# Latent products on unshifted input, with the shift's row added by matmuls, and new orders in conv norm, gathers and the last up unit

## What is computed

```
ada = silu(c) @ w_ada + b_ada;  sh_m, sc_m, ... = split(ada, 6)     # rows of 1024
h   = rmsnorm(x, g) * (1 + sc_m) + sh_m
cq, ckv, k_rope, fq, fk, fv, f_logit, g_mla, g_fox = split(h @ w_in)
q = rmsnorm(cq) @ w_uq;  kv = rmsnorm(ckv) @ w_ukv                   # the latents, 384 and 256 wide
```

## Time and profile before

| | us |
|---|---|
| median of 3 runs (lowest, highest) | 1018.14 (1015.21, 1019.87) |
| the profiled execution | 1018.16 |
| its span, first to last instruction | 1016.4 |
| TensorE matmuls busy | 965.3 (95%) |
| VectorE (DVE) busy | 465.0 (46%) |
| ScalarE (ACT) busy | 378.7 (37%) |
| mean granted TensorE clock | 0.986 |
| read from memory | 307.31 MB, 303 GB/s over the span |

### The profile page before, as it was taken

The page is one execution under the profiler, slowest core; times in us unless marked ns, Lnnn a source line. Parts: engine busy times, 40 slices in busy tenths (PEclk is TensorE's granted clock), DMA queues, the critical chain, the costliest instruction groups (busy, mean ns, idle before and its releaser), DMA issues.

```text
span 1016.4 us, 15018 instructions
## 1 busy us (share of the span) xinstructions
PE 965.3 (95%) x6185; PEld 668.1 (66%) x6185; DVE 465.0 (46%) x858; ACT 378.7 (37%) x718; POOL 27.4 (3%) x60
## 2 busy tenths in 40 slices
PE   6899999998999999999989899999999999998997
PEld 3698777898999999987988534343434443332433
DVE  1787666575688468757784411212121212111113
ACT  2455545464666356553672422121211121111211
POOL 1000000000000000002121000000000000000000
PEclk9999999999999999989999999999999999999999
DMA  9967733452655445444575599999999999999996
GB/s 386 390 261 268 293 153 158 173 241 83 247 193 216 175 166 193 173 173 166 189 310 232 226 428 429 426 428 427 427 430 427 427 428 427 429 426 427 428 427 269
DMA packets 23397, 309.34 MB, mean 304 GB/s; under 512 B 2592, under 2 KB 3104, under 8 KB 4000
## 3 DMA queue, kind: packets, MB, share of 16 engines
q1 hardware_dynamic: 23184, 307.32, 74.1%
q10 hardware_dynamic: 144, 1.05, 0.3%
HBM read 307.31 MB, written 1.05 MB: 303 GB/s over the span
## 4 chain that ended last, share of the span: by engine, by line
PE 79%; DMA 14%; DVE 5%; issue 1%; ACT 1%; POOL 0%; DVEq 0%; SPq 0%
PE ps L996 76%; DMA ring<-experts 4%; DMA work<-experts 4%; DMA slot<-experts 4%; DMA ring<-dense 2%; DVE wl L1638 1%; PE ps L1194 1%; PE ps L1565 1%; DVE ring L1722 0%; PE ps L1507 0%; DVE xT L2065 0%; DVE wb L2142 0%; ACT wh L577 0%; PE ps L1159 0%; PE ps L1319 0%
## 5 line engine op out<-in xcount | busy, mean ns | idle before, releaser
L996 PE MATMUL ps<-hH,wh 128*128 128x256 f32 x704 | 201.3, 286 | 4.0 <-DVE hL L1662 1.9
L1638 DVE TENSOR_TENSOR wl<-ring,wh 128x1024 fp32r<-128x1024 f32 (+1 forms) x136 | 163.9, 1215 | 85.2 <-ACT wh L577 84.8
L996 PE MATMUL ps<-hL,wh 128*128 128x256 f32 x704 | 198.9, 283 | 0.0
L996 PE MATMUL ps<-hH,wl 128*128 128x256 f32 x704 | 198.8, 282 | 0.0
L577 ACT ACTIVATE wh<-ring 128x1024 fp32r<-128x1024 f32 (+1 forms) x136 | 140.8, 1044 | 125.3 <-PE ps L996 99.3
L996 PEld LDWEIGHTS ps<-hH,wh 128*128 128x128 f32 x704 | 134.6, 191 | 6.1 <-issue 3.7
L996 PEld LDWEIGHTS ps<-hL,wh 128*128 128x128 f32 x704 | 134.4, 191 | 0.0
L996 PEld LDWEIGHTS ps<-hH,wl 128*128 128x128 f32 x704 | 134.2, 191 | 0.0
L2334 DVE SCALAR_TENSOR_TENSOR wc<-wc,w_slot,ps 128x512 f32<-128x512 f32 x16 | 12.0, 747 | 220.9 <-PE ps L996 220.9
L996 PE MATMUL ps<-aH,wh 128*128 128x256 f32 x304 | 86.1, 283 | 5.9 <-DVE wb L2190 2.6
L996 PE MATMUL ps<-aL,wh 128*128 128x256 f32 x304 | 85.3, 281 | 0.0
(11 more groups left out here) (349 smaller groups left out, 1419.4 us busy)
## 6 DMA issues: line engine op xcount, KB each, us to landing
ring<-dense SPq DMA_DIRECT2D x39, 2048.0 KB, 8.1
ring<-experts SPq DMA_DIRECT2D x28, 2048.0 KB, 27.8
slot<-experts SPq DMA_DIRECT2D x28, 2048.0 KB, 28.9
work<-experts SPq DMA_DIRECT2D x20, 2048.0 KB, 28.2
early<-experts SPq DMA_DIRECT2D x10, 2048.0 KB, 26.5
wb<-experts SPq DMA_DIRECT2D x9, 2048.0 KB, 25.2
early<-dense SPq DMA_DIRECT2D x4, 2048.0 KB, 9.2
ring<-dense SPq DMA_DIRECT2D x4, 1024.0 KB, 4.7
```

The lines of the kernel that those rows point to most:

```text
L996: return nc.tensor.matmul(o_, l, r, start=start, stop=stop, skip_group_check=True)
L1638: V.tensor_tensor(wl[:, c % CHUNKS, 0:n], src, wh[:, c % CHUNKS, 0:n].bitcast(F32), ALU.subtract)\
```

## The change

- The shift's ada items are loaded after cq and ckv. These two are multiplied with the parts of n_t without the shift, which go to aH and aL; the shift's ada products are done between ckv's chunks. Then shift_product multiplies the shift's columns with the raw weights of cq and of ckv (in four groups of columns), ACT copies the row (shift_row), and shift_add multiplies it with a matrix of ones into the accumulators, which adds the sum over the four groups to every token. The slots of cq and ckv are kept until then.
- fq accumulates in banks 4 and 5, and the shifted hH and hL are made beside the first chunks of fq. DVE's order of ada steps and splits is new up to uq1: the last two steps of ada12 come after uq1's split.
- Scale's and shift's ada products use four groups of 256 columns instead of two of 512, and half the columns are copied and turned.
- Conv norm: the product with the gate, the squares, their mean and the spread come earlier in the orders of DVE, ACT and TensorE; the last w2o_attn chunk stands behind the spread.
- The fourth gather is done after unit 0; unit 93 is loaded in two transfers, each with half the rows of every product, and the second half of it is awaited only in the middle. Two semaphores are merged into one (dve_setup).

```diff
+LAST_UP = PER_PASS - 3
...
+SHIFT_STEPS = {"cq": 1, "ckv": 3}
...
-    for nm, c0, k0, kn, slot in (("scale0", D, 0, 4, None), ("scale1", D, 4, 4, None), ("shift0", 0, 0, 4, 4),
-                                 ("shift1", 0, 4, 2, 5), ("shift2", 0, 6, 2, TAIL)):
+    def ada_cols_item(nm, c0, k0, kn, slot=None):
         item(f"ada_{nm}", kn, D, [("w_ada", k0, c0, D)], 0, None, slot)
+
+    ada_cols_item("scale0", D, 0, 4)
+    ada_cols_item("scale1", D, 4, 4)
     in_item("cq", 0)
     in_item("ckv", 2)
-    in_item("fq", 0)
+    ada_cols_item("shift0", 0, 0, 4, 4)
+    ada_cols_item("shift1", 0, 4, 2, 5)
+    ada_cols_item("shift2", 0, 6, 2, TAIL)
+    in_item("fq", 4)
...
+        shift_rows = {"cq": wa[:, 2048:2048 + Q_RANK], "ckv": wa[:, 2048 + Q_RANK:2048 + CKQ + HEADS]}
...
+            def half_k(v, i):
+                return v.rearrange("p (j n) -> p j n", j=2)[:, :, 1024 * i:1024 * i + 1024]
+
             def load_unit(u):
-                if u < PER_PASS - 1:
+                if u == LAST_UP:
+                    for i in range(2):
+                        sp.dma_start(half_k(unit(u), i), half_k(W["experts"][u], i))\
+                            .then_inc(unit_loaded(u, 0)[0] if i else S(f"slot{TAIL}_loaded"), 16)
...
+                    if before["name"] in SHIFT_STEPS:
+                        sp.wait_ge(S("shift_steps"), SHIFT_STEPS[before["name"]])
...
-                if i == 0:
-                    act.wait_ge(S("ada_cols"), 1)
-                norm_high(0, adaT[:, SH_M:SH_M + KD], 2 * i, 2 * i + 2)
+                for k in (2 * i, 2 * i + 1):
+                    act.wait_ge(S("norm_t"), k + 1)
+                    nc.scalar.activation(aH[:, k, :], n_t[:, k, :], ACT.Copy).then_inc(S("norm_high"), 1)
             split("ckv")
-            split("fq", 0, 2)
+            split("fq", 0, 1)
+
+            def shift_row(name, steps):
+                act.wait_ge(S("shift_steps"), steps)
+                nc.scalar.activation(shift_rows[name], ps[:, 7, 0:IT[name]["n"]], ACT.Copy).then_inc(S("shift_row"), 1)
+
+            act.wait_ge(S("ada_cols"), 1)
+            norm_high(0, adaT[:, SH_M:SH_M + KD], 0, 4)
+            split("fq", 1, 2)
+            shift_row("cq", 1)
+            norm_high(0, adaT[:, SH_M:SH_M + KD], 4, 8)
+            split("fq", 2, 3)
+            shift_row("ckv", 3)
+            split("fq", 3)
 
             act.wait_ge(S("lat_copied"), 4)
...
-            split("fq", 2)
...
+            act.wait_ge(S("cy_ready"), 2)
+            nc.scalar.activation(csq, cy, ACT.Square).then_inc(S("cv_sq"), 1)
             o2_out(2)
             squares_o2(3)
             split("w2o_attn", 2, 3)
-            act.wait_ge(S("cy_ready"), 2)
-            nc.scalar.activation(csq, cy, ACT.Square).then_inc(S("cv_sq"), 1)
...
-            def ada_half(name, row):
+            def ada_half(name, c0):
 
                 it = IT[f"ada_{name}"]
                 pe.wait_ge(S(f"slot{it['slot']}_loaded"), it["loaded"])
                 w = slot_view(it)
                 for kk in range(it["kn"]):
                     k = it["srcs"][0][1] + kk
-                    for q in range(2):
-                        r = 32 * (row + q)
-                        ins = mm(ps[r:r + 1, 7, :], cact[:, k:k + 1], w[:, kk, 512 * q:512 * q + 512], k == 0, k == KD - 1)
+                    for q in range(4):
+                        ins = mm(ps[32 * q:32 * q + 1, 7, c0:c0 + 256], cact[:, k:k + 1], w[:, kk, 256 * q:256 * q + 256],
+                                 k == 0, k == KD - 1)
                 ins.then_inc(S("ada_used"), 1)
 
             def turn_half(i):
                 pe.wait_ge(S("ada_row"), i + 1)
-                for s in range(4):
-                    r = slice(64 * i, 64 * i + 64)
-                    ins = nc.tensor.transpose(ps[:, 6, 256 * i + 64 * s:256 * i + 64 * s + 64], ada_row[r, s * P:s * P + P],
-                                              ident[r, r])
+                for s in range(2 * i, 2 * i + 2):
+                    ins = nc.tensor.transpose(ps[:, 6, s * P:s * P + P], ada_row[:, s * P:s * P + P], ident[:])
                 ins.then_inc(S("ada_turned"), 1)
...
-            pe.wait_ge(S("bank7_zero"), 1)
+            pe.wait_ge(S("dve_setup"), 1)
             ada_half("scale0", 0)
             norm_totals(0, 5)
             ada_half("scale1", 0)
             norm_spread("norm_rstd", 1, rstd, 4)
             turn_half(0)
-            for i in range(3):
-                ada_half(f"shift{i}", 2)
+
+            def shift_product(name):
+
+                it = IT[name]
+                for k in range(KD):
+                    q = k % 4
+                    ins = mm(ps[32 * q:32 * q + 1, 7, 0:it["n"]], adaT[:, SH_M + k:SH_M + k + 1], slot_view(it)[:, k, :],
+                             k < 4, k >= 4)
+                ins.then_inc(S("shift_steps"), 1)
+
+            def shift_add(name, count):
+
+                it = IT[name]
+                pe.wait_ge(S("shift_row"), count)
+                for tt in range(TT):
+                    ins = mm(ps[:, it["acc"] + tt, 0:it["n"]], ones, shift_rows[name], False, True)
+                ins.then_inc(S("shift_steps"), 1)
+
+            linear("cq", aH, aL, True, ready=("norm_in", [IN_BASE[0] + k + 1 for k in range(KD)]))
+            pe.wait_ge(S("c_steps"), 3)
+            chunk("ckv", 0, aH, aL, True)
+            ada_half("shift0", 256)
+            chunk("ckv", 1, aH, aL, True)
+            ada_half("shift1", 256)
+            ada_half("shift2", 256)
+            chunk("ckv", 2, aH, aL, True)
             turn_half(1)
-
-            linear("cq", hH, hL, True, ready=("norm_in", [IN_BASE[0] + k + 1 for k in range(KD)]))
-            pe.wait_ge(S("c_steps"), 3)
-            linear("ckv", hH, hL, True)
-            pe.wait_ge(S("lat_copied"), 2)
-            linear("fq", hH, hL, False)
-            pe.wait_ge(S("lat_copied"), 4)
-            pe.wait_ge(S("fz_in"), 1)
+            chunk("ckv", 3, aH, aL, True)
+            h_in = ("norm_in", [IN_BASE["shifted"] + k + 1 for k in range(KD)])
+            pe.wait_ge(S("ada_cols"), 1)
+            shift_product("cq")
+            chunk("fq", 0, hH, hL, False, ready=h_in)
+            shift_add("cq", 1)
+            shift_product("ckv")
+            chunk("fq", 1, hH, hL, False, ready=h_in)
+            shift_add("ckv", 2)
+            for ci in range(2, 4):
+                chunk("fq", ci, hH, hL, False, ready=h_in)
+            pe.wait_ge(S("lat_copied"), 5)
             linear("fk", hH, hL, False)
+            linear("fv", hH, hL, True)
...
+            chunk("w2o_attn", 3, aH[:, 4:8], aL[:, 4:8], False, 0, True, False, o_in)
...
+                    if u == LAST_UP:
+                        pe.wait_ge(S(f"slot{TAIL}_loaded"), base_loaded[TAIL] + p * 16 + 16)
+                    else:
+                        pe.wait_ge(*unit_loaded(u, p))
                     w = unit(u)
                     for kk in range(4):
                         k = 4 * half + kk
+                        if u == LAST_UP and kk == 2:
+                            pe.wait_ge(*unit_loaded(u, p))
...
+                    if u == 0:
+                        gather(0, 3, FIRST_BANKS[3])
 
             def put(tt, c0, n, bank):
 
...
-                for i in range(4):
+                for i in range(3):
...
-                r = slice(64 * i, 64 * i + 64)
                 dve.wait_ge(S("ada_used"), count)
-                V.tensor_copy(ada_row[r], ps[r, 7, :]).then_inc(S("ada_row"), 1)
+                V.tensor_copy(ada_row[:, 256 * i:256 * i + 256], ps[:, 7, 256 * i:256 * i + 256]).then_inc(S("ada_row"), 1)
...
-            half_out(1, IT["ada_shift2"]["ada"]).then_inc(S("ada_cols"), 1)
-            dve.wait_ge(S("ada_cols"), 1)
             for i in range(4):
                 split("cq", i, i + 1)
                 for k in (2 * i, 2 * i + 1):
                     dve.wait_ge(S("norm_high"), IN_BASE[0] + k + 1)
+                    V.tensor_tensor(aL[:, k, :], n_t[:, k, :], aH[:, k, :].bitcast(F32), ALU.subtract).then_inc(S("norm_in"), 1)
+            split("ckv")
+            split("fq", 0, 1)
+            half_out(1, IT["ada_shift2"]["ada"]).then_inc(S("ada_cols"), 1)
+            dve.wait_ge(S("ada_cols"), 1)
+            for i in range(4):
+                for k in (2 * i, 2 * i + 1):
+                    dve.wait_ge(S("norm_high"), IN_BASE["shifted"] + k + 1)
                     V.scalar_tensor_tensor(out=hL[:, k, :], in0=n_t[:, k, :], scalar=adaT[:, SH_M + k:SH_M + k + 1],
                                            in1=hH[:, k, :].bitcast(F32), op0=ALU.add, op1=ALU.subtract).then_inc(S("norm_in"), 1)
-            split("ckv", 0, 2)
+                if i < 3:
+                    split("fq", i + 1, i + 2)
+            dve.wait_ge(S("shift_steps"), 2)
+            for tt in range(TT):
+                V.tensor_copy(cqkv[:, tt, 0:Q_RANK], ps[:, IT["cq"]["acc"] + tt, 0:Q_RANK]).then_inc(S("lat_copied"), 1)
             dve.wait_ge(S("c_steps"), 3)
```

(49 more changed lines are left out.)

19 lines of the change are left out of this document (8 added, 11 removed).

## The result

The changed kernel took 1028.57 us by the median of four runs (1026.17 to 1031.60), the kernel before beside it 1018.67: 1.0122 times as long, with a 95% interval of 1.0097 to 1.0147. The forecast was 1023.2, the range ended at 1028.0. The profiled execution is the shortest of the four, 1026.17 us with a span of 1024.4, so 8.0 longer than the profile before; the medians are 9.9 apart. This gap between profile and median turns out to matter.

What follows compares the result with a forecast made beforehand. The prediction took the chain of waits to end in the stream of expert weights, moved by any delay upstream of unit 0. 2.0 + 8.5 - 0.4 - 2.9 - 0.95 - 1.2 = +5.05 on 1018.16: 1023.2 us, range 1013.5 to 1028.

Steps and rivals of the forecast that it cites:

- part 2: DVE order: ada(1,2)'s last steps behind uq1's split issue ada13, ukv1 and g0 late: +8.5 us, 0.4 given back.
- part 1: Start: cq begins 9.3 us earlier, but 11.3 us are added on TensorE before fv's end: +2.0 us there.
- part 3: Conv norm: cy is multiplied earlier on DVE, so w2o_conv starts earlier: -2.9 us (-1.5 to -4).
- part 4: Gathers: gather 3 moves behind unit 0, so unit 0 ends and the weight stream restarts earlier: -0.95 us.
- added on TensorE up to fv's end, clock left out: Before fv's end: shift products 3.7, turn 0.4, new products and adds 4.7, fk 0.85 us.
- clock after the gap: TensorE idles from about 22.7 to 27.6 us ahead of cq; the lower clock then loses 1.6 us.
- Rival 1: Loads from 92 to 112 us: the late ada13 is covered, the DVE-order term nearly vanishes; 1015 us, chance 0.13.
- rival 3: ada13, ukv1, g0 and ada20 share the queue's rate, ada13 comes 3 to 5 us later; 1026 to 1028, chance 0.15.
- fk's wait: Before fv's end: DVE copies latents after the shift's addition, so fk's split is late: 0.85 us, between 0 and 2.
- cq ran at full rate after near idle: Lower bound of 0 for the clock loss ahead of cq, from 3 us of near idle at 34 to 36.9 us.
- Part 5: Last up unit: it lands in halves, TensorE starts earlier, unit 94's landing then limits: -1.2 us (0 to -1.6).

Runs made afterwards that it cites:

- ada12_early: The changed kernel with the last two ada(1,2) steps directly behind the first two, ahead of uq0's and uq1's splits: 1020.98 us, ratio 1.0036 to the kernel before.
- last_alone: The kernel before with only the last up unit's load in halves: 1016.42 us against 1017.71, ratio 0.9997.
- conv_alone: The kernel before with the conv-norm change alone: 1016.02 us against 1017.71, ratio 0.9985.
- four_groups_conv_last: The kernel before with ada products on four column groups, the conv-norm change and the last up unit in halves: 1012.97 us against 1017.03, ratio 0.9962.
- gather_alone: The kernel before with only gather 3 moved behind unit 0: 1016.41 us against 1017.71, ratio 0.9994.
- after_again: The changed kernel run once more without an edit: 1027.63 us against 1017.40 for the kernel before, ratio 1.0099.

## Why the prediction was right and wrong

The mechanism of the largest term was right, and so was its size: part 2 decides, the end goes the slow way. What failed are sizes in the other parts, all to the same side: the start (part 1) came out at +4.8 us instead of +2.0, conv norm (part 3) at -1.1 instead of -2.9, the gathers (part 4) at +0.4 instead of -0.95.

| term | forecast | measured |
|---|---|---|
| cq's first matmul | 27.6 | 26.6 to 29.7, mean of four 28.1 |
| the same against before | -9.3 | -7.2 (before: mean of five 35.3) |
| added on TensorE up to fv's end, clock left out | 9.65 | 10.6 (59.72 less 49.1) |
| clock after the gap | 1.6 | 1.7 to 2.7 (61.4 to 62.4 less 59.72) |
| fv's end | +2.0 | +2.4 by the two profiles, +4.8 by the means (90.18 of three, 85.36 of five) |
| ada13, ukv1, g0 late | +8.5 - 0.4 | +8.1 (40.17 less 32.10) |
| conv norm | -2.9 | -1.84, and +0.75 at the gathers |
| gather 3 | -0.95 | +0.4 |
| last up unit | -1.2 | -0.9 |

- **Part 2** came out step by step. Forecast and the profile after: ada13 issued near 95 and at 95.41, DVE's wait 5 to 6 and 5.75 us, g0 ready for ACT at about 109.5 and at 109.37, its first matmul near 112.5 and at 112.52. From fv's end to that matmul it was 8.1 us more than before (24.13 against 16.05), where 8.5 was forecast. ada12_early takes most of it back. The rule on ring order that the prediction took from the Trainium skill, "DMA: Bandwidth & Descriptors", section "Queues, rings and completion order", speaks of the order in which descriptors are taken up, not of landing; "can't pass" said more than it. The landings did keep the order: ada13 was there for DVE at 103.22, ukv1 for ACT at 104.50, g0 at 109.37. Rival 1 is out, and rival 3 too: ada13 did not come later than 8 us after its issue.
- **Part 1** is the largest miss, 2.8 us at fv's end by the means, and it has three pieces. The first, 1.8 us, is the sum of the added work and the clock, forecast at 11.3 and measured at 13.1 (62.2 from cq to fv in the three profiles, less 49.1 at full rate). The work came to 10.6 instead of 9.65, by small excesses in nearly every part: two shift products at 1.9 each (3.7 forecast for both), their turn 0.4, the product rows 1.47 and 1.18 (1.4 and 1.05), the adds 1.45 and 1.16 (1.3 and 1.0, by 3.45 us for an expert unit, where two units start 3.47 apart), fk's wait 1.00 (0.85). That is 10.5 of the 10.6. The clock cost 2.1 to 2.7 in these three profiles instead of 1.6.
- The second piece, 0.6 us, is the baseline. I wrote that the profiled execution and the median "stand for each other", which held for the whole time, 1018.16 and 1018.14, and not for its stages. Of five profiles with the old start this one had the latest cq, 36.87 against a mean of 35.3; its scale0 took 5.07 us (5.47 in last_alone, 3.60 in the other three). It made up for most of that with a cq at full rate, which three of the five didn't have: its fv ended at 85.95 against a mean of 85.36. So the bound "cq ran at full rate after near idle", which I took from it, was one of two outcomes of the same code. The third piece, 0.4 us, is cq's own start, 28.0 in the mean of the three profiles instead of 27.6. That the first profile after had its cq at 26.61 was luck: by it alone the start seemed to cost 2.4.
- **Part 3**: the wait for cy fell from 2.62 to 0.55 us and the wait on aL went, as forecast. I priced GpSimd's power at 2.90, from a row in which VectorE's split began 0.12 us behind it, though the change puts it behind the start of a split: 0.91 of the 1.06 us that were missing. Two rows of the changed kernel show the rest of the chain, TensorE's wait and GpSimd's power:

```profile
550.25 1.97 PE L1027 MATMUL ps<-ident,rstd 128*64 128x128 f32 x32 [1.22 <-POOL rstd L551]
```

```profile
546.39 3.81 POOL L551 TENSOR_TENSOR rstd<-ms,minus_half 128x16 f32<-128x16 f32 x1 [3.73 <-DVE ms L2143]
```

- And 0.75 of the gain is given back behind the router: with the new conv norm u10 is issued 10.0 us behind the first gather, without it 9.2 to 9.3. More of the gathers' matmuls run at half clock. conv_alone and four_groups_conv_last have it both, so it belongs to conv norm. The traces show how: in all twelve profiles without filling products ahead of the gathers, the granted clock is back at its upper level 103.2 to 103.6 us behind the matmul near 470 us, with the old conv norm and with the new one. The gathers now begin 1.7 to 1.9 us earlier behind that matmul, and the clock's return doesn't move with them. The forecast put this at nothing. The stretch from 3.8 to 5.2 us behind the first gather shows it, in last_alone (old conv norm) and in conv_alone; why the return doesn't move stays open:

```profile
571.93:573.33 1.40, 1.40 (x14) 1.40 (x14) 0.00 (x0) 1.27 (x4) 0.00 (x0) 1.00 0.00 0
571.38:572.78 1.40, 1.40 (x8) 1.40 (x8) 0.00 (x0) 0.83 (x2) 0.00 (x0) 0.50 0.00 0
```

- **Part 4**: I took unit 0's end for the restart of the stream. The stream is paced by the second slot too: u10 came 0.93 earlier in gather_alone, nearly as forecast, and the load behind it waited for unit 1, which came later by the two changes of form. In the changed kernel the issues are at 587.63 and 592.36, 4.73 apart; before 3.44:

```profile
587.63 0.33 SPq L453 DMA_DIRECT2D early<-experts  x1
592.36 0.33 SPq L453 DMA_DIRECT2D work<-experts  x1
```

- **Part 5**: right in kind, unit 94's landing is late next, 0.82 in the profile after; in after_again that landing was later still (1.35) and nothing was won.

```profile
1011.10 3.65 PE L1027 MATMUL ps<-slot,wc 128*64 128x512 f32 x16 [0.82 <-DMA slot<-experts]
```

With the measured terms: 4.8 + 8.1 - 1.84 + 0.75 + 0.4 - 0.9 = +11.3 us, against +10.2 (after_again) and +9.9 (the first runs) by the medians. The executions of one kernel differ by 3 to 9 us themselves, and up to 3 of that lie between scores and 471 us (350.1 to 353.0 in all fourteen profiles), which no part touches.

## What to carry to other kernels

When a step that releases a buffer is moved on its engine, follow the release through the in-order queue of loads: here two additions behind one split moved three loads and cost 7 us, and one line gave them back. Read the stages of a baseline from several executions, not one, when TensorE's clock changes inside them; a total that agrees with the median says nothing of its parts. A duration read from a row holds for the order of its neighbours too: look at what the other engine was doing when it began. And take the cheap half of a change first: four column groups without the reordering, with conv norm and the last unit, took 0.996 of the time of before, where the whole change took 1.012.

## What the runs showed of the hardware

- Products of the identity in an idle stretch kept the clock at its upper level: cq's first 24 matmuls took 4.07 us instead of 5.77, 2.4 us of the time by the medians; ahead of the gathers, u10 2.3 us earlier. The same filling ahead of a cq that was bound by a load won nothing.
- Ahead of the gathers the clock's return to its upper level came 103.2 to 103.6 us behind a matmul near 470 us in twelve profiles, whether the gathers began 97.9 to 98.2 or 99.6 to 99.8 us behind it: work won there was in part paid back at half rate.
- The first ada product, 16 or 32 instructions at a recorded clock of 1.00, took 3.60 or 5.07 to 5.47 us with two column groups and 1.91 or 3.3 to 3.5 with four, from one execution to the next. The record of the clock doesn't explain it; it is open.
- GpSimd's power over 16 columns: 3.81 us when a VectorE split was running as it began, 2.90 when none was, also with a split that began 0.12 us later; the later split wasn't held up.
- The same start, with the same two idle stretches of 0.80 and 1.74 us ahead of cq, left cq at full rate in two profiles and at half rate for a while in two others (four kernels that differ only later): 4.06 and 5.63 us for 24 matmuls.
